# Two stages of a fused transformer block: the weight remainders of one input projection move from VectorE to GpSimd, and a depthwise convolution reads an SBUF copy instead of PSUM

## The reference

```python
def conv_ffn(h, w_up, taps, conv_b, w_down, rows):
    a, g = jnp.split(h @ w_up, 2, axis=-1)                 # 2816 value and 2816 gate channels
    g2, tp = g.reshape(bsz, rows, GRID_W, f), taps         # 256 tokens as 4 rows of 64
    gc = lax.conv_general_dilated(g2, tp[:, :, None, :], (1, 1), 'SAME', ...)   # 3x3, depthwise
    gc = gc.reshape(bsz, t, f) + conv_b
    return (a * jax.nn.gelu(gc, approximate=False)) @ w_down

# second block
h = modulate(rmsnorm_2(x, norm_mix[l]), sh1, sc1)
p = h @ w_in[l]            # PROJ_WIDTH = 3584: seven blocks of 512
# block 6 is gelu'd and layer-normed per head (v); blocks 0 and 1 become log-sigmoid gates
```

## Time and profile before

| | us |
|---|---|
| median of three executions | 2004.6 |
| the profiled execution | 2004.6 |
| its span, first to last instruction | 2002.8 |
| PE busy (share of the span) | 1879.4 (94%) |
| DVE busy | 1234.1 (62%) |
| ACT busy | 919.8 (46%) |
| POOL busy | 642.6 (32%) |
| mean granted TensorE clock | 0.972 of full speed |

### The profile page before, as it was taken

How to read it: one execution, slowest core, us unless ns; L and a number is a source line. 1 busy time by engine, 2 the same in 40 slices (tenths; PEclk the granted TensorE clock), 3 DMA queues, 4 the chain that set the end, 5 groups by cost and what they waited for, 6 DMA issues and landing times.

```text
span 2002.8 us, 33369 instructions
## 1 busy us (share of the span) xinstructions
PE 1879.4 (94%) x11448; PEld 1597.9 (80%) x11448; DVE 1234.1 (62%) x2242; ACT 919.8 (46%) x1279; POOL 642.6 (32%) x305
## 2 busy tenths in 40 slices
PE   6999887999899999999999999999998999889996
PEld 5998866895765889999999988888873765549996
DVE  2476775641411399457767588888872657637776
ACT  4556624442433644467777533333342552214443
POOL 5887523784331688810000000000000013103333
PEclk9999988999999999999999999999998999989998
DMA  5554301457433457665555777777776532225553
GB/s 183 189 181 163 130 22 55 157 186 240 142 137 124 139 177 214 205 185 175 172 175 177 221 253 238 238 237 237 237 252 217 175 95 94 85 105 179 183 184 105
DMA packets 121684, 343.41 MB, mean 171 GB/s; under 512 B 13776, under 2 KB 46672, under 8 KB 121360
## 3 DMA queue, kind: packets, MB, share of 16 engines
q1 hardware_dynamic: 120096, 335.32, 51.8%
q0 software_dynamic: 1520, 7.21, 1.0%
HBM read 324.65 MB, written 17.83 MB: 171 GB/s over the span
## 4 chain that ended last, share of the span: by engine, by line
PE 62%; POOL 3%; DVE 2%; issue 2%; ACT 2%; DMA 0%; POOLq 0%; DVEq 0%; ACTq 0%
PE banks L842 61%; POOL weight_rest L738 3%; ACT weight_high L1378 1%; ACT arena L1378 0%; DMA weight_ring<-in_stream 0%; PE banks L853 0%; DVE act_feature_major L1833 0%; DVE arena L2375 0%; DVE act_feature_major L1836 0%; ACT scratch L1378 0%; ACT L1378 0%; DVE residual L2348 0%; DVE arena L2346 0%; DVE weight_rest L2172 0%; POOLq L379 0%
## 5 line engine op out<-in xcount | busy, mean ns | idle before, releaser
L1378 ACT ACTIVATE weight_high<-weight_ring 128x1024 fp32r<-128x1024 f32 x436 | 460.8, 1057 | 459.9 <-PE banks L842 416.7
L738 POOL TENSOR_TENSOR weight_rest<-weight_ring,weight_high 128x1024 fp32r<-128x1024 f32 x204 | 520.7, 2559 | 239.2 <-ACT weight_high L1378 121.3
L2172 DVE TENSOR_TENSOR weight_rest<-weight_ring,weight_high 128x1024 fp32r<-128x1024 f32 x232 | 284.0, 1225 | 177.9 <-ACT weight_high L1378 170.6
L842 PE MATMUL banks<-a_high,weight_high 128*128 128x256 f32 x1216 | 306.0, 289 | 4.3 <-DVE a_rest L1848 4.1
L842 PE MATMUL banks<-a_rest,weight_high 128*128 128x256 f32 x1216 | 299.9, 284 | 0.0
L1378 ACT ACTIVATE arena<-banks 128x512 f32<-128x512 f32 (+4 forms) x262 | 172.9, 681 | 165.4 <-PE banks L842 163.3
L842 PEld LDWEIGHTS banks<-a_high,weight_high 128*128 128x128 f32 x1216 | 234.4, 193 | 5.0 <-issue 4.5
L842 PEld LDWEIGHTS banks<-a_rest,weight_high 128*128 128x128 f32 x1216 | 235.0, 193 | 0.2 <-issue 0.2
L842 PE MATMUL banks<-weight_high,gated_high 128*128 128x512 f32 x512 | 201.5, 394 | 0.0
L842 PE MATMUL banks<-weight_high,gated_rest 128*128 128x512 f32 x512 | 200.3, 391 | 0.0
L842 PE MATMUL banks<-a_high,weight_rest 128*128 128x256 f32 x1216 | 173.6, 286 | 12.4 <-POOL weight_rest L738 12.4
(11 more groups left out here) (292 smaller groups left out, 3251.6 us busy)
## 6 DMA issues: line engine op xcount, KB each, us to landing
weight_ring<-in_stream SPq DMA_DIRECT2D x504, 512.0 KB, 3.5
arena<-in_stream SPq DMA_DIRECT2D x66, 512.0 KB, 3.3
unit_spill<-small SPq DMA_DIRECT2D x128, 128.0 KB, 3.6
scratch<-unit_spill SPq DMA_DIRECT2D x128, 128.0 KB, 3.2
residual<-in_x SPq DMA_DIRECT2D x2, 512.0 KB, 4.3
arena<-in_mem POOLq DMA_DIRECT2D x2, 512.0 KB, 4.7
arena<-in_ctx POOLq DMA_DIRECT2D x2, 512.0 KB, 5.0
arena<-in_keys POOLq DMA_DIRECT2D x1, 1024.0 KB, 5.1
```

Of the source, the lines that this page charges most:

```text
L738: nc.gpsimd.tensor_tensor(w_lo[:, e % 2, :], raw(e)[0], w_hi[:, e % 2, :], ALU.subtract).then_inc(S["rest_ready"], 1)
L842: return nc.tensor.matmul(out, lhsT, rhs, start=start, stop=stop, skip_group_check=True)
L1378: return nc.scalar.activation(out, in_, f, **kw)
L2172: tt(w_lo[:, e % 2, :], raw(e)[0], w_hi[:, e % 2, :], ALU.subtract).then_inc(S[ready], 1)
```

## The change

**Input projection.** GpSimd now writes all 28 rests: tile `I0` before it issues two constant loads, the other 27 behind them, in one row (semaphore `rest_ready`). VectorE's 28 rests go, and its layer norm and gate operations stand one behind the other.

**Feed-forward.** ScalarE copies each gate from PSUM to a new SBUF area `GC`, right behind the centre tap, and that copy frees the bank. The eight taps on VectorE read `GC` instead of PSUM. The rest of the next gate tile stands between the sixth and the seventh tap instead of behind the eighth (`meanwhile`). The gelu waits for a semaphore of the last tap (`ffn_conv`) instead of for the bank, and its call moves over the loop's edge; the order gelu, gate, three high copies stays.

```diff
@@ rest_count
+            if e < I0:
+                return S["lo_ready"], e - UD + 1
+            return S["rest_ready"], UD + e - I0 + 1
@@ areas
+        GC = area(18432, 2, T)
@@ block.gpsimd
+            def in2_rest(e):
+                pool.wait_ge(S["hi_ready"], e + 1)
+                pool.wait_ge(S["hi_begun"], e)
+                nc.gpsimd.tensor_tensor(w_lo[:, e % 2, :], raw(e)[0], w_hi[:, e % 2, :],
+                                        ALU.subtract).then_inc(S["rest_ready"], 1)
+
+            in2_rest(I0)
             arrived(pool, ("x2T", 1, 1))
             pool.dma_start(WSP, A["wsp"]).then_inc(in_second, 16)
             pool.dma_start(GSPAN, A["span"]).then_inc(in_second, 16)
+            for e in range(I0 + 1, F0):
+                in2_rest(e)
@@ block.scalar, ffn_gate
                 func(CV[:, par, :], b, ACT.Identity, scale=col("taps")[:, bass.ds(c * 9 + 4, 1)],
-                     bias=col("fconv_b")[:, bass.ds(c, 1)]).then_inc(S["ffn_center"], 1)
-
-            def ffn_gelu(job, par, turn=None):
-                freed(act, job, turn)
+                     bias=col("fconv_b")[:, bass.ds(c, 1)])
+                free(func(GC[:, par, :], b, ACT.Copy), job)
+
+            def ffn_gelu(c, par):
+                act.wait_ge(S["ffn_conv"], c + 1)
                 func(GE[:, par, :], CV[:, par, :], ACT.Gelu).then_inc(S["ffn_gelu"], 1)
...
-            ffn_gelu(("g0",), 0)
             with act.Fori(0, (FC - 2) // 2) as i:
                 for u in range(2):
+                    ffn_gelu(i * 2 + u, u)
                     ffn_gate(("ga", 2 * u), i * 2 + (u + 1), (u + 1) % 2, i)
...
-                    ffn_gelu(("ga", 2 * u), (u + 1) % 2, i)
@@ block.vector, input projection
-            split_rest(I0, "lo_ready")
...
-            in2_rests(1, 6)
-            projected(6)
+            for b in P_ORDER:
+                for t in range(TT):
+                    freed(dve, ("p", b, t))
+                if b == 6:
...
+                if b == 1:
+                    gate_logs(PJ[:, :, 0:1024], LF, K2, ("g_abs", "g_l", "g_nk", "g_logf"))
@@ block.vector, conv_channels
-                dve.wait_ge(S["ffn_center"], c + 1)
+                freed(dve, gate_job, turn)
                 tap = lambda k: col("taps")[:, bass.ds(c * 9 + k, 1)]
-                x, o = grid(arrived(dve, gate_job, turn)[:, 0:T]), grid(CV[:, par, :])
+                x, o = grid(GC[:, par, :]), grid(CV[:, par, :])
...
-                    if k < 8:
-                        ins.then_inc(step.c.sem, 1)
-                    else:
-                        free(ins, gate_job)
+                    ins.then_inc(step.c.sem if k < 8 else S["ffn_conv"], 1)
+                    if n == 5 and meanwhile:
+                        meanwhile()
```

More of the change, by code:

```diff
@@ L461, in build @@
             g_k g_kd g_H z_made z_pool dve_columns ctx_e o_ms o_root v_ms v_root rows_used v_ready
-            oc_ready gdiag x3_ready ffn_center ffn_gelu x4_ready out_ready act_step dve_step zeros_ready
+            oc_ready gdiag x3_ready ffn_conv ffn_gelu x4_ready out_ready act_step dve_step zeros_ready
             neg_a m_hi_ready m_lo_ready at_hi_ready at_lo_ready y_hi_ready y_lo_ready mg_hi_ready
@@ L503, in rest_count @@
                 return S["rest_ready"], e + 1
-            return S["lo_ready"], e - UD + 1
+            if e < I0:
+                return S["lo_ready"], e - UD + 1
+            return S["rest_ready"], UD + e - I0 + 1
         def bank(name):
@@ L1794, in _ @@
                     split_high(F0 + 6 + 3 * u, i, 6, (S["ffn_down_lo_ready"], i * 2 + (u + 1)))
-                    ffn_gelu(("ga", 2 * u), (u + 1) % 2, i)
+            ffn_gelu(FC - 2, 0)
             ffn_gate(("ge",), FC - 1, 1)
@@ L1798, in _ @@
             split_high(F0 + 65, rests=(S["ffn_lo_ready"], 44))
-            ffn_gelu(("ge",), 1)
+            ffn_gelu(FC - 1, 1)
             norm(9, lambda t: hres[:, t, :], lambda t: XN[:, t, :], lambda t: act.wait_ge(S["x4_ready"], 4))
@@ L2228, in _ @@
             O, VV = PJ[:, :, 0:512], PJ[:, :, 3072:3584]
[L2229 to L2236, removed]
-            in2_rests(1, 6)
-            projected(6)
-            step(V.tensor_reduce(gst[:, 3, 1], h4(VV), AX.X, ALU.add))
-            step(ts(gst[:, 3, 1], gst[:, 3, 1], 1.0 / P, None, ALU.mult))
@@ L2242, in _ @@
[L2242 to L2269, removed]
+            for b in P_ORDER:
+                for t in range(TT):
+                    freed(dve, ("p", b, t))
+                if b == 6:
+                    step(V.tensor_reduce(gst[:, 3, 1], h4(VV), AX.X, ALU.add))
+                    step(ts(gst[:, 3, 1], gst[:, 3, 1], 1.0 / P, None, ALU.mult))
+                    step(tt(h4(VV), h4(VV), bc(gst[:, 3, 1], 3, P), ALU.subtract))
+                    step(tt(SQV, VV, VV, ALU.mult))
+                    step(V.tensor_reduce(gst[:, 0, 1], h4(SQV), AX.X, ALU.add))
+                    signal(ts(gst[:, 1, 1], gst[:, 0, 1], 1.0 / P, EPS, ALU.mult, ALU.add), "v_ms")
+                    dve.wait_ge(S["v_root"], 1)
+                    step(V.reciprocal(gst[:, 3, 1], gst[:, 2, 1]))
+                    step(tt(h4(VV), h4(VV), bc(gst[:, 3, 1], 3, P), ALU.mult))
+                    dve.wait_ge(in_second, 4 * 16)
+                    step(tt(VV, VV, bc(R2[:, 512:1024], 1, TT), ALU.mult))
+                    signal(tt(VV, VV, bc(R2[:, 1024:1536], 1, TT), ALU.add), "v_ready")
+                if b == 1:
+                    gate_logs(PJ[:, :, 0:1024], LF, K2, ("g_abs", "g_l", "g_nk", "g_logf"))
@@ L2362, in _, with conv_channels @@
                 split_rest(F0 + r, "ffn_lo_ready")
-            def conv_channels(gate_job, c, base, par, turn=None):
-                dve.wait_ge(S["ffn_center"], c + 1)
+            def conv_channels(gate_job, c, base, par, turn=None, meanwhile=None):
+                freed(dve, gate_job, turn)
                 tap = lambda k: col("taps")[:, bass.ds(c * 9 + k, 1)]
-                x, o = grid(arrived(dve, gate_job, turn)[:, 0:T]), grid(CV[:, par, :])
+                x, o = grid(GC[:, par, :]), grid(CV[:, par, :])
                 for n, k in enumerate((0, 1, 2, 3, 5, 6, 7, 8)):
@@ L2393, in _ @@
             per = 7
-            conv_channels(("g0",), 0, n0, 0)
-            split_rest(F0 + 2, "ffn_lo_ready")
+            conv_channels(("g0",), 0, n0, 0, meanwhile=lambda: split_rest(F0 + 2, "ffn_lo_ready"))
             split_rest(F0 + 3, "ffn_lo_ready")
@@ L2399, in _ @@
                 for u in range(2):
-                    conv_channels(("ga", 2 * u), i * 2 + (u + 1), i * (2 * per) + (n0 + per * (u + 1)), (u + 1) % 2, i)
-                    split_rest(F0 + 5 + 3 * u, "ffn_lo_ready", i, 6)
+                    conv_channels(("ga", 2 * u), i * 2 + (u + 1), i * (2 * per) + (n0 + per * (u + 1)), (u + 1) % 2, i,
+                                  lambda: split_rest(F0 + 5 + 3 * u, "ffn_lo_ready", i, 6))
                     split_rest(F0 + 6 + 3 * u, "ffn_lo_ready", i, 6)
```

## The result

| | before | after |
|---|---|---|
| median of five executions each, us | 2004.6 | 2027.42 |
| range, us | 2003.05 to 2012.79 | 2026.17 to 2028.88 |
| profiled execution, its span, us | 2004.6, 2002.8 | 2026.23, 2024.4 |

The ratio is 1.0109, 95% interval 1.009 to 1.0129: slower by 22.8 us, where 52 us were forecast, with a range that began at 2035 us. The direction and the place were right, the size was not.

A forecast was written before the change was run, and what follows sets the result against it. TensorE bounds the kernel now, but the exclusion with GpSimd would make VectorE the feed-forward bound: 2004.6 us + 45 (feed-forward) + 7.2 (input projection) = 2056.8, given as 2057 us, range 2035 to 2077 us.

The forecast's parts named there:

- the exclusion by whole instructions: Both stages: VectorE with two SBUF operands and GpSimd wait for each other's whole instruction; one operand in PSUM avoids it.
- VectorE's group as 7.39 + 2.42 + 0.73 + 0.06 = 10.6 us: Feed-forward: VectorE's work plus GpSimd's two rests and handovers exceeds 8.5 us, +2.1 us a group, +45 us with the end.
- The lower bound: Feed-forward: if only GpSimd's long rest blocks, 1.3 us a group, 27 us; the total range began at 2035 us.
- The order "only": Feed-forward: moving the first rest between the taps changes only the order, no sum of VectorE's time.
- The tail: Feed-forward, last group: 1 us more, counted within the +45 us.
- The copy at 0: Feed-forward: ScalarE's gate copy is hidden if VectorE is the bound, cost 0; otherwise up to 10 us.
- The table load at 0: Feed-forward loop: gelu's table load of 1.28 us, ten here, falls where ScalarE idles, cost 0; behind the taps' signal 13 us.
- The input projection: +7.2 forecast: Projection: GpSimd's rests run late through VectorE's norm and gate operations and ScalarE's pauses, +7.2 us; bounds +1.2 and +13 us.
- The signs: Profile after: VectorE busy over 95% of feed-forward, taps near 2.8 and 1.1 us, ten table loads with nobody behind them.
- No exclusion: Rival, both stages: exclusion does not reach these instructions; 2006 to 2022, say 2010 us; chance 0.12.
- Lower clock: Rival, feed-forward: the waits also lower TensorE's clock, 29 us more, 2086 us; chance 0.09.
- TensorE slowed by PSUM reads: Rival, feed-forward: VectorE's PSUM reads slow TensorE's 256-column matmuls; removing them gains 7.0 us, 1997.6 us; chance 0.03.

The follow-up runs named there:

- e3: Kernel before plus ScalarE's gate copy, which nobody reads, and the first rest between the sixth and seventh tap; taps still read PSUM: 2007.34 us, ratio 1.0018.
- e9: Kernel before with only the first rest moved between the sixth and seventh tap; no copy, taps from PSUM: 2003.06 us, ratio 1.0003.
- e5: Feed-forward edit alone, with GpSimd's rest of the down tile cut from 1024 to 8 columns: 2002.66 us, ratio 0.9989.
- e11: Feed-forward edit alone, with the rest of the down tile on VectorE between the third and fourth tap instead of GpSimd: 2007.26 us, ratio 1.0011.
- e7: Feed-forward edit alone, with GpSimd's rest of the down tile written by four instructions of 256 columns: 2030.22 us, ratio 1.0141.
- e4: Feed-forward edit alone, with both weight rests back behind the eighth tap: 2041.41 us, ratio 1.0185.
- e1: Kernel before with the input projection edit alone, feed-forward part as before: 2009.02 us, ratio 1.003.
- e2: Kernel before with the feed-forward edit alone, projection as before: 2023.24 us, ratio 1.0094.
- e8: Projection edit alone, with the layer norm's five operations on 128x1024 cut to a few columns, value block not normalized: 2009.15 us, ratio 1.003.

## Why the prediction was right in direction and wrong in size

- **What bounds the kernel, and the exclusion by whole instructions: right.** Taps from SBUF stand still beside GpSimd, taps from PSUM don't (e3, e9), and without GpSimd's long rest the others don't either (e5) or only beside the hidden rest (e11, 0.37 us a group). That is the rule that I had from the Trainium skill, "GPSIMD Engine Reference", section "Key points", at the length that the earlier trace rows gave it. The advice of the Trainium skill's other page, "VectorE: DVE Perf Modes", section "Rules for kernel authors" (copy to SBUF first), brought no shorter tap: 0.41 us from either.
- **The step that failed: VectorE's group as 7.39 + 2.42 + 0.73 + 0.06 = 10.6 us. It measures 9.25 us.** Three parts of this sum were too large.
  1. The standstill was taken as GpSimd's recorded time, 3.15 us; it is 2.17 us. Some 0.3 to 0.4 us of each GpSimd instruction's row holds nobody: in the projection a norm operation of 1.22 us takes 3.31 us beside a rest of 2.40 us, so 2.09 us of hold. And inside the loop each hold swallows some 0.1 us of the gap that VectorE leaves between two taps anyway. The last group, which lies outside the loop and has smaller gaps, shows it: its eight taps take 3.71 us before and 6.08 us after, 2.37 us more, against 2.17 us inside for the same two holds. That the whole deduction of some 0.48 us is fixed and no share of the row is borne out by e7 (0.73 - 0.48 = 0.25 us a quarter); how it divides into the two parts is an inference from this one pair.
  2. "Moving the first rest between the taps changes no sum of VectorE's time" was false: 7.39 became 7.08 us, because the rest fills a gap. e4 measures it.
  3. The handovers' 0.06 us were not there.
  
  Together 0.98 + 0.31 + 0.06 = 1.35 us a group, some 27 us over 20 groups. Also, 20 intervals ran at the new period, not 21: the first is 6.15 us, shorter than its 6.65 us before.
- **The lower bound failed for the same reason.** "Only the long rest blocks" gave 1.3 us a group with the recorded 2.42 us and the 7.39 us; 0.74 us was measured. The ends of the range were also added up otherwise than worked out: the lower took 4 us for the projection, whose own bound was 1.2 us, the upper 58 us where the text has 60. By the text's own bounds they would be 2033 and 2078 us, and 2027 us lies below them too. The earlier trace rows held a better end: there a tap-sized operation stood for 2.39 - 0.42 = 1.97 us, which is what e4 shows (2.00 us).
- **The order "only": its cost missed altogether.** I saw VectorE's 1.11 us of idle as room. It was the slack of a loop, and without the moved rest the feed-forward edit costs 37 us (e4). Its 10.15 us are near my 10.6 by coincidence: another mechanism, not the sum of works.
- **The tail: +4.4 us against 1 us.** TensorE stands still once for 3.5 us:

```profile
PE banks L854 <- POOL hidden_rest L838: 3.5, 1, 3.5
```

  The last group's taps have hardly any matmuls left to hide them, so their 2.37 us of standstill come late in full; before, that wait was 0.9 us. Behind that wait the last twelve matmuls run at a granted clock of 0.50 (the lower level, 1.2 GHz; before 1.00 at the same place) and stand 0.43 us apart in place of 0.23 us, which makes 1.7 of the 4.4 us. One of them after, and one before:

```profile
2005.94 0.63 PE L854 MATMUL banks<-weight_high,hidden_high 128*128 128x512 f32 x1
```

```profile
1985.24 0.40 PE L842 MATMUL banks<-weight_high,hidden_high 128*128 128x512 f32 x1
```

  e11 waits 3.6 us there as well, and that is most of what it loses.
- **The copy at 0: right as the text had it, and so was its condition.** With VectorE as the bound it is hidden; where VectorE is not (e3), it costs 3.4 us, inside the bound of 10 us.
- **The table load at 0: right.** It stands behind the last high copy, and ScalarE then still waits for the taps (start us, us, operation, idle before):

```profile
1880.05 1.06 ACT L1390 ACTIVATE weight_high<-arena 128x1024 fp32r<-128x1024 f32 x1 [1.80 <-POOL weight_rest L832]
1881.13 1.28 ACT L1390 ACT_TABLE_LOAD   x1
1884.04 0.42 ACT L1390 ACTIVATE arena<-arena 128x256 f32<-128x256 f32 x1 [1.63 <-DVE arena L2365]
```

- **The input projection: +7.2 forecast, +6.3 measured within the stage, +5.0 us in e1's time.** GpSimd's rests and the norm alternate as described. Tile 13's rest part came 4.1 us late, not 5.1. Of the six operations five held GpSimd for 0.24 to 0.29 us less than their own rows; the sixth fell mostly into 1.30 us in which GpSimd waited for a high copy, a wait that the forecast's unbroken row did not have. In the timeline of GpSimd eight rests in a row take 23.25 us where eight times 2.40 would be 19.2 us; two of the norm's operations beside them:

```profile
1572.50 23.25 POOL L803 TENSOR_TENSOR weight_rest<-weight_ring,weight_high 128x1024 fp32r<-128x1024 f32 x8 [1.30 <-ACT weight_high L1390]
```

```profile
1573.00 3.29 DVE L2256 TENSOR_TENSOR arena<-arena 128x1024 f32<-128x1024 f32 x1
1576.33 3.31 DVE L2257 TENSOR_TENSOR arena<-arena 128x1024 f32<-128x1024 f32 x1
```

- **The signs.** VectorE was busy for 91% of the stage (98.86 of 109 us), not over 95%; the long and the middling tap took 2.33 and 0.67 us in place of 2.8 and 1.1; the ten table loads are there with nobody behind them.
- **Rivals.** No exclusion: refuted. Lower clock: refuted for the loop (1.00); only the end of the stage has it, for 1.7 us. TensorE slowed by PSUM reads: e5, with taps from SBUF, has 8.50 us against 8.52 us in e9; the gain would be 0.4 us in all, not 7.

**Open.** 1.7 us of the 2.4 us that came back between the stages lie in one row: 16 matmuls at span 1648 take 7.03 us where they took 8.73 us before, at a granted clock of 1.00 against 0.80. The short row stands in all three profiles with the projection edit and in e2, the long one in the eight others; whether the edit brings it is not settled.

## What to carry to other kernels

When a VectorE operation changes from one SBUF operand to two, look at what GpSimd does at that moment. Size the standstill by an operation that already stood still in the trace, not by GpSimd's row, and count it once for each GpSimd instruction. Before calling an engine's idle time room, follow what ends it: if the chain comes back to the same engine, it is the slack of a loop, and one instruction placed earlier in the loop can be worth more than the work that is saved.

## What the runs showed of the hardware

- The exclusion takes some operations with one tensor operand too, however small: in the projection a TENSOR_SCALAR of 128x8, 0.17 us when free, took 2.10 us beside a rest. It doesn't take all: in e8 a TENSOR_REDUCE over 128x1024 in SBUF kept its 1.22 us inside a rest of GpSimd (1564.55 to 1566.95), which kept its 2.40 us. The two rows, from the changed kernel and from e8:

```profile
1560.09 2.10 DVE L2247 TENSOR_SCALAR mixer_stats<-mixer_stats 128x8 f32<-128x8 f32 x1
```

```profile
1564.70 1.22 DVE L2248 TENSOR_REDUCE mixer_stats<-arena 128x8 f32<-128x1024 f32 x1
```

- The hold goes back and forth at instruction boundaries: four pieces of 256 columns let a tap through after each, and hold 1.07 us in all where one piece of 1024 holds 2.00 us (e4).
- In a hardware loop dependent taps start 0.55 to 0.63 us apart at 0.41 to 0.48 us each, and outside it eight take 3.71 us in place of 4.46 us: some 0.1 us a tap, which I put down to the register rows that stand between the taps only in the loop.
